# Two expert weight loads issued in five pieces each instead of one

## The reference

```python
def expert_choice_ffn(x, w_router, w_gate_up, w_down):
    B, T, D = x.shape
    cap = EC_CAPACITY_FACTOR * T // N_EXPERTS          # 2 * 512 // 16 = 64
    logits = jnp.einsum('btd,de->bte', x, w_router, preferred_element_type=jnp.float32)
    aff = jax.nn.softmax(logits, axis=-1)
    gate, idx = lax.top_k(jnp.swapaxes(aff, 1, 2), cap)
    bidx = jnp.arange(B)[:, None, None]
    xs = x[bidx, idx]
    h = jnp.einsum('becd,edf->becf', xs, w_gate_up)    # 16 experts, 1024 x 2048
    hg, hu = jnp.split(h, 2, axis=-1)
    ye = jnp.einsum('becf,efd->becd', jax.nn.silu(hg) * hu, w_down)   # 16 experts, 1024 x 1024
    ye = ye * gate[..., None].astype(ye.dtype)
    return jnp.zeros_like(x).at[bidx, idx].add(ye)
```

## Time and profile before

| what | value |
|---|---|
| time, median of 3 runs | 2116.12 us (2115.82 to 2117.74) |
| the profiled execution, its own time | 2118.99 us |
| its span, first to last instruction | 2117.1 us |
| TensorE busy | 2086.5 us (99%) |
| VectorE, ScalarE, GpSimd busy | 1022.9, 749.9 and 146.3 us |
| bytes moved by DMA | 352.09 MB, mean 166 GB/s |

### The profile page before, as it was taken

The page is one execution under the profiler, slowest core; times in us unless marked ns, Lnnn a source line. Parts: engine busy times, 40 slices in busy tenths (PEclk is TensorE's granted clock), DMA queues, the critical chain, the costliest instruction groups (busy, mean ns, idle before and its releaser), DMA issues.

```text
span 2117.1 us, 24858 instructions
## 1 busy us (share of the span) xinstructions
PE 2086.5 (99%) x10137; PEld 1518.3 (72%) x10137; DVE 1022.9 (48%) x1515; ACT 749.9 (35%) x1076; POOL 146.3 (7%) x149
## 2 busy tenths in 40 slices
PE   9999999999999999999999999999999999999998
PEld 7878888888777778888888877777788544444433
DVE  7875433444666664434446656565464312122123
ACT  7774322323455542222234456433332100011012
POOL 0220000001000020000001010072100000000000
PEclk9999999999999999999999999999999999999999
DMA  6233223223211122232233322242236999999996
GB/s 218 73 107 107 84 83 125 93 75 115 76 61 56 64 90 100 75 119 101 82 86 123 117 53 75 67 86 76 75 108 234 401 426 413 426 427 426 426 427 277
DMA packets 88944, 352.09 MB, mean 166 GB/s; under 512 B 9472, under 2 KB 24064, under 8 KB 64512
## 3 DMA queue, kind: packets, MB, share of 16 engines
q1 hardware_dynamic: 83856, 342.48, 43.4%
q0 software_dynamic: 2192, 2.63, 1.0%
q10 hardware_dynamic: 2784, 5.41, 0.7%
HBM read 347.06 MB, written 2.10 MB: 165 GB/s over the span
## 4 chain that ended last, share of the span: by engine, by line
PE 87%; DVE 5%; DMA 4%; ACT 3%; issue 2%; POOL 0%; SPq 0%; ACTq 0%; DVEq 0%; POOLq 0%
PE PS L2197 20%; PE PS L2199 19%; PE PS L2198 19%; PE PS L2604 9%; PE PS L2644 5%; DMA SL<-in_wgu_dram 3%; PE PS L2240 2%; DVE WL L1677 1%; PE PS L2314 1%; PE PS L2588 1%; PE PS L2338 1%; PE PS L2328 1%; PE PS L2589 1%; DVE XC L1744 1%; PE PS L2436 1%
## 5 line engine op out<-in xcount | busy, mean ns | idle before, releaser
L2197 PE MATMUL PS<-HH,WH 128*128 128x512 f32 x1392 | 554.4, 398 | 4.0 <-DVE HL L1717 1.9
L2199 PE MATMUL PS<-HH,WL 128*128 128x512 f32 x1392 | 543.8, 391 | 0.0
L2198 PE MATMUL PS<-HL,WH 128*128 128x512 f32 x1392 | 543.0, 390 | 0.0
L1677 DVE TENSOR_TENSOR WL<-RAW,WH 128x1024 fp32r<-128x1024 f32 (+4 forms) x302 | 343.6, 1138 | 294.1 <-ACT WH L1351 293.2
L1351 ACT ACTIVATE WH<-RAW 128x1024 fp32r<-128x1024 f32 (+4 forms) x302 | 286.4, 950 | 308.5 <-PE PS L2199 278.3
L2197 PEld LDWEIGHTS PS<-HH,WH 128*128 128x128 f32 x1392 | 261.9, 188 | 69.3 <-issue 10.3
L2199 PEld LDWEIGHTS PS<-HH,WL 128*128 128x128 f32 x1392 | 261.7, 188 | 55.5
L2198 PEld LDWEIGHTS PS<-HL,WH 128*128 128x128 f32 x1392 | 262.1, 188 | 53.2 <-issue 1.0
L2604 PE MATMUL PS<-SL,XS 128*64 128x512 f32 x928 | 220.8, 595 | 6.5 <-DMA SL<-in_wgu_dram 5.8
L2604 PEld LDWEIGHTS PS<-SL,XS 128*64 128x64 f32 x928 | 70.5, 137 | 135.7 <-issue 133.7
L2199 PE MATMUL PS<-MH,WL 128*128 128x512 f32 x352 | 137.1, 389 | 0.0
(11 more groups left out here) (375 smaller groups left out, 2741.8 us busy)
## 6 DMA issues: line engine op xcount, KB each, us to landing
SL<-in_wgu_dram SPq DMA_DIRECT2D x116, 1024.0 KB, 21.9
SL<-in_wdn_dram SPq DMA_DIRECT2D x55, 1024.0 KB, 24.7
RAW<-in_w_dram SPq DMA_DIRECT2D x46, 512.0 KB, 3.5
RAW<-in_wg_dram SPq DMA_DIRECT2D x44, 512.0 KB, 3.4
RAW<-in_wu_dram SPq DMA_DIRECT2D x44, 512.0 KB, 3.4
RAW<-in_wd_dram SPq DMA_DIRECT2D x32, 384.0 KB, 3.0
RAW<-in_wqkv_dram SPq DMA_DIRECT2D x24, 512.0 KB, 3.4
RAW<-in_wd_dram SPq DMA_DIRECT2D x32, 320.0 KB, 2.8
```

The lines of the kernel that those rows point to most:

```text
L1677: e.tensor_tensor(wl, raw, wh.bitcast(F), ALU.subtract).then_inc(*wlo.did("u", u))
L2197: e.matmul(out, wh[:, w], xh, start=k == 0, stop=False)
L2198: e.matmul(out, wh[:, w], xl, start=False, stop=False)
L2199: m = e.matmul(out, wl[:, w], xh, start=False, stop=k == g.total - 1)
```

## The change

The up-projection loads 124 and 132 are no longer one issue over 128 partitions but five issues: partitions 0 to 95 in one, and then 96 to 103, 104 to 111, 112 to 119 and 120 to 127 in one each. The bytes, the buffers, the order and the waits stay; the semaphore of the buffer rises by 80 instead of 16 for such a load, and TensorE waits for the whole sum.

```diff
+UNEVEN = (124, 132)
...
-                if i < len(loads) - 4:
+                if i in UNEVEN:
+                    for p0, p1 in ((0, 96), (96, 104), (104, 112), (112, 120), (120, 128)):
+                        e.dma_start(SL[j][p0:p1, :], src[p0:p1]).then_inc(*d_slot[j].did(i))
+                elif i < len(loads) - 4:
                     e.dma_start(SL[j][:, :], src).then_inc(*d_slot[j].did(i))
```

## The result

The changed kernel takes 2128.12 us (median of 6 runs, 2126.53 to 2131.2) against 2117.31 us before (6 runs): +10.8 us, a ratio of 1.0052 with a 95% interval of 1.0042 to 1.0062. It is slower by half a per cent, and by more than the forecast range allowed. The prediction had given 0.17 to a loss of more than 4.2 us. The profiled execution took 2127.87 us, its span is 2126.1 us, 9.0 us more than before.

A forecast was written before the change was run, and what follows sets the result against it. The weight stream on the sixteen DMA engines was taken to bound the kernel's end. More rows on a last engine add 1.2 us, SP's issues nothing: 2116.1 + 1.2 = 2117.3 us, range 2114.8 to 2122 us.

The forecast's parts named there:

- The bound: At the kernel's end, the weight stream decides: making the last load land x later lengthens the kernel by x.
- Eight engines, always the same: In the small pieces: each uses eight engines, the same eight for all four, giving those 10 rows a load, others 6.
- SP's own time: Issuing on SP: eight more issues at 0.43 us are 3.5 us, hidden by buffer waits and costed at nothing.
- What a small piece really costs: In the eight-partition pieces: the unknown, taken as the engine's own pace of 0.31 us a row.
- pieces that queue at their partitions: Rival for the narrow pieces: eight engines writing eight partitions at once queue there; +2 to +12 us, chance 0.25.
- the upper third: The part of the queueing rival's +2 to +12 us that the forecast range, ending at 2122 us, left out.
- six rows on each engine: In the 96-partition issues: spread over sixteen engines, each moves six rows at 0.31 us instead of eight.
- The balance term of 1.23 us: At the stream's end: both uneven loads put 1.23 us more on eight engines and 1.23 us less on the others.
- the sign that was chosen: At the stream's end: a more loaded engine is last, so slower, +1.2 us, chance 0.42; the trace left the sign open.
- Three instruction packets: In the DMA queues, 1900 to 1960 us: 16 KB packets each hold an engine as long as two rows, making ends uneven.
- the 1.6 us that it could give: At the stream's end: idle area per engine, the most that perfect balance of the bytes could gain.

The follow-up runs named there:

- the small ones alone: The changed kernel with partitions 0 to 95 of loads 124 and 132 left out, only the four eight-partition pieces issued: +2.6 us over before, ratio 1.0011.
- The balance kernel: Against the change: first 6 KB of all 128 rows in one issue, last 2 KB in sixteen pieces of every fourth partition; +5.9 us over before, 1.0025.
- the two with 96 and spread pieces: The change with small pieces taking every fourth partition, of 96 to 127 (high, +11.8 us over before) or of 0 to 31 (low, +9.0 us).
- The early pair: The change with loads 20 and 28 in five pieces instead of 124 and 132: +9.0 us over before, ratio 1.0049.
- low, spread pieces: Against the change: first 4 KB of all rows in one issue, last 4 KB of partitions 0 to 63 in eight every-fourth pieces, rest omitted; 0.0 us, 0.9997.
- the dear high ones: As the low, spread pieces, but on partitions 64 to 127, the last 4 KB of 0 to 63 left out: +3.9 us over before, ratio 1.0019.
- the one load: The change with only load 124 in five pieces and load 132 in one: +6.2 us over before, ratio 1.0031.
- low, neighbouring pieces: As the low, spread pieces, but each writes eight neighbouring partitions: +3.6 us over before, 1.0014; with source rows read spread, +3.0 us, 1.0010.

## Why the prediction was wrong

**The bound, right.** The end hangs on the stream one for one. In the table the lost time and the measured time agree within 1.2 us for eleven of the fifteen kernels. Of the other four, the left-out rows explain the small ones alone. The balance kernel and the two with 96 and spread pieces are 2.7 to 3.3 us above their lost time, but the execution traced was the fastest of each: it took 9.7, 7.7 and 4.5 us more than the median before (high, low, balance), where the lost time and 1.2 us of balance make 10.1, 7.5 and 3.8. The early pair shows that loads in hand don't hide a loss, only a pause of the stream does: 9.9 us lost, 1.9 given back and 1.2 of balance make 9.2, and 9.0 were measured. The prediction had loads 124 and 132 in hand by 9 to 10 us and rightly gave that no credit beyond their own place.

**Eight engines, always the same, right as far as the runs show.** 64 tiny packets more; and the free low, spread pieces beside the dear high ones fit if the eight are always those of partitions 0 to 63.

**SP's own time, nothing, right.** Ten issues along the row instead of two: ratio 1.0001. The issues of the changed kernel took 0.64 us and not 0.43, but that is 2 us more for all ten, and SP still waits 81 us for buffers between 1890 and 2060.

**The step that failed: "What a small piece really costs".** It took the engine's own pace, 0.31 us a row, because the 8 KB row on the same queue was the nearest row. That row is of a load over all 128 partitions, and a narrow piece gives this up. The mean row is 0.56 us in the first part of a hole and 0.85 to 1.15 us where the small pieces run, which is past the 0.7 us from which the prediction saw a loss of over 4.2 us. The small pieces alone lose 4.9 us of the stream. The rival that had it, pieces that queue at their partitions, was given 0.25 and +2 to +12 us, and its sign came true: the rate falls under 427 GB/s between 1925 and 1960 us, and TensorE's waits grow with the end. The time came at +10.8, in the part of it that the range left out. That part, +6 to +12 us, was called the upper third and is three fifths of its span.

**A second step that failed: "six rows on each engine".** The piece over 96 partitions was costed at 6 x 0.31 us and no rival doubted it, as it uses all sixteen engines. It alone loses 6.2 us, more than the small pieces. Its own rows at 0.56 us would explain only half of that (12 x 0.25 = 3.0 us for both loads). Four pieces of 32 lose 7.7 us. The rival spoke of eight engines only, so even it had the place of the cost half wrong; its price for both loads, up to 12 us, was near by way of another sum, and that is luck.

**Who is slowed.** The prediction had the eight more loaded engines late and the others early. In the trace the other eight are slow in the hole as well. That is why the loss is near 5 us a load and not the 0.61 us of balance.

**The balance term of 1.23 us** is small beside it, and the times can't tell whether it is there. With it, the change's 10.0 us lost make 11.2, and 10.8 were measured; the one load's 5.5 and 0.6 make 6.1, and 6.2 were measured; but each interval is about 2 us wide to either side. The ends of the streams fit late engines on both halves, and so the sign that was chosen, without showing it.

**A reading that was off.** Three instruction packets take 0.3% of 16 x 60 us, about 1 us each, so they hold an engine as long as three rows do, not two. That they make the end uneven was argued and not tested.

**Still open:** why all sixteen engines slow down together, to a mean of 1.15 us a row, when only eight of them work on the small pieces; why the large piece costs the stream twice what its own rows explain. The way that a 96-partition piece is dealt to the engines was not seen, only its effect.

## What to carry to other kernels

In a stream that keeps the DMA engines busy throughout, as this one, cut a load along its rows and keep all 128 partitions in every piece: five such pieces cost nothing, five pieces along the partitions cost 5 us a load. Before taking the price of a transfer from a row of the trace, ask not only for its size and queue but for which partitions it fills and who else fills them at that time. And in the trace, look at the rate beside the share: a share of 1.0 at less than the usual rate for rows of the same size was the mark of every slow piece here. Pieces on eight engines were free on partitions 0 to 63 and cost 3.9 us on 64 to 127, so a balance between the engines that needs such pieces on the high half costs more than the 1.6 us that it could give.

## What the hardware showed that was not expected

- Pieces of 96 and 32 partitions slow the stream to 160 to 250 GB/s for 6 to 8 us at each load, though all sixteen engines take part.
- While pieces of eight neighbouring partitions between 96 and 127 move on eight engines, the others slow down too: 1.15 us in the mean for a row of 8 KB instead of 0.31, 115 GB/s instead of 427.
- Pieces on eight engines cost nothing when they are spread over partitions 0 to 63: 0.0 us for sixteen such pieces.
- Reading the rows spread instead of as neighbours made no difference to low, neighbouring pieces: 2.8 against 2.7 us lost.
